# Loading the memory and the first weight unit in alternating column halves, with products of zeros on TensorE until the memory is there

## What is computed

```python
kv_m = rms_norm(mem, mem_norm_g[l]) @ w_mem_kv[l]
k_m, v_m = jnp.split(kv_m, 2, axis=-1)
...
h = rms_norm(x, norm_g[l])
proj = h @ w_in[l]
```

## Time and profile before

| | |
|---|---|
| median of 3 executions | 1388.79 us (1387.9 to 1390.12) |
| the profiled execution's own time | 1389.63 us |
| its span, first to last instruction | 1387.8 us |
| PE, DVE, ACT, POOL busy | 1349.3, 971.3, 742.3, 57.0 us |
| mean granted TensorE clock | 0.997 |
| HBM read | 224.05 MB |

### The profile page before, as it was taken

The page is one execution under the profiler, slowest core; times in us unless marked ns, Lnnn a source line. Parts: engine busy times, 40 slices in busy tenths (PEclk is TensorE's granted clock), DMA queues, the critical chain, the costliest instruction groups (busy, mean ns, idle before and its releaser), DMA issues.

```text
span 1387.8 us, 17865 instructions
## 1 busy us (share of the span) xinstructions
PE 1349.3 (97%) x7119; PEld 1146.4 (83%) x7119; DVE 971.3 (70%) x1230; ACT 742.3 (53%) x1045; POOL 57.0 (4%) x46
## 2 busy tenths in 40 slices
PE   7999999989999999999999999999999999999998
PEld 6978888978887898887877888879888887788886
DVE  6689776699776498747876555457796678565644
ACT  6864766764684565544454444346744444454432
POOL 1002000001100001000000000000100000000000
PEclk9999999999999999999999999999999999999999
DMA  8554335544343655434445554455643344476553
GB/s 294 186 169 155 100 122 182 183 129 155 113 144 131 224 176 174 147 126 144 152 152 182 182 182 168 166 180 185 200 157 123 120 143 146 145 221 186 189 180 110
DMA packets 139697, 226.25 MB, mean 163 GB/s; under 512 B 8096, under 2 KB 54880, under 8 KB 139488
## 3 DMA queue, kind: packets, MB, share of 16 engines
q1 hardware_dynamic: 137952, 222.49, 48.8%
q10 hardware_dynamic: 1664, 2.63, 0.5%
HBM read 224.05 MB, written 1.05 MB: 162 GB/s over the span
## 4 chain that ended last, share of the span: by engine, by line
PE 80%; DVE 12%; ACT 4%; issue 2%; POOL 1%; DMA 0%; SPq 0%; ACTq 0%; DVEq 0%
PE gp L613 61%; PE gp L602 7%; PE mp L585 4%; DVE arena L1466 4%; DVE wt_rest L1472 3%; PE mp L896 2%; PE mp L715 1%; DVE arena L1472 1%; PE mp L782 1%; DVE arena L1956 1%; POOL rs_out L2222 1%; DVE arena L1469 1%; PE mp L757 1%; ACT arena L1048 1%; PE mp L743 0%
## 5 line engine op out<-in xcount | busy, mean ns | idle before, releaser
L1472 DVE TENSOR_TENSOR wt_rest<-wt,wt_hi 128x1024 fp32r<-128x1024 f32 x156 | 184.1, 1221 | 77.6 <-ACT wt_hi L1080 76.9
L1080 ACT ACTIVATE wt_hi<-wt 128x1024 fp32r<-128x1024 f32 x156 | 156.8, 1054 | 101.9 <-DMA wt<-in_ffn_up 51.0
L1080 ACT ACTIVATE mix_hi<-wt 128x1024 fp32r<-128x1024 f32 x136 | 139.7, 1062 | 103.3 <-PE gp L613 58.4
L1472 DVE TENSOR_TENSOR wt_rest<-wt,mix_hi 128x1024 fp32r<-128x1024 f32 x136 | 160.5, 1220 | 34.2 <-ACT mix_hi L1080 33.3
L613 PE MATMUL gp<-wt_rest,mix_hT_hi 128*128 128x512 f32 x384 | 149.8, 390 | 0.0
L613 PE MATMUL gp<-mix_hi,mix_hT_hi 128*128 128x512 f32 x352 | 140.7, 400 | 4.6 <-DVE wt_rest L1472 3.7
L613 PE MATMUL gp<-wt_hi,hT_hi 128*128 128x512 f32 x352 | 140.2, 398 | 4.8 <-DVE wt_rest L1472 4.0
L613 PE MATMUL gp<-wt_hi,hT_rest 128*128 128x512 f32 x352 | 137.5, 391 | 0.0
L613 PE MATMUL gp<-mix_hi,mix_hT_rest 128*128 128x512 f32 x352 | 137.3, 390 | 0.0
L613 PE MATMUL gp<-wt_rest,hT_hi 128*128 128x512 f32 x352 | 137.2, 390 | 0.0
L1080 ACT ACTIVATE first_hi<-wt 128x1024 fp32r<-128x1024 f32 x104 | 106.4, 1061 | 49.1 <-PE gp L613 36.7
(11 more groups left out here) (331 smaller groups left out, 2913.7 us busy)
## 6 DMA issues: line engine op xcount, KB each, us to landing
wt<-in_w_in SPq DMA_DIRECT2D x100, 1024.0 KB, 5.0
wt<-in_ffn_gate SPq DMA_DIRECT2D x44, 512.0 KB, 4.0
wt<-in_ffn_up SPq DMA_DIRECT2D x44, 512.0 KB, 5.0
wt<-in_w_out SPq DMA_DIRECT2D x20, 1024.0 KB, 5.0
wt<-in_ffn_down SPq DMA_DIRECT2D x20, 1024.0 KB, 5.1
wt<-in_w_mem_kv SPq DMA_DIRECT2D x8, 1024.0 KB, 6.2
wt<-in_w_branch_pool SPq DMA_DIRECT2D x4, 1024.0 KB, 5.1
wt<-in_w_branch_ret SPq DMA_DIRECT2D x4, 1024.0 KB, 5.0
```

What stands on the lines that cost most here:

```text
L1080: nc.scalar.activation(rounded_part(u)[:, k:k + nk, :], wt[:, u % SLOTS, k:k + nk, :], ACT.Copy)\
L1472: return nc.vector.tensor_tensor(o, i0, i1, ALU.subtract)
```

## The change

SP loads the memory as two column halves of both tiles and unit 0 as two half units, in the order memory half 0, weight half 0, memory half 1, weight half 1. A new semaphore first_part stands for weight half 0. The steps memT0 to memT3 are renumbered (q, t) = divmod(i, 2) on all engines. DVE handles column half 0 fully (two multiplications, then remainder of memory, weight half 0, remainder of memory, weight half 1) ahead of column half 1. ACT rounds weight half 0 ahead of the second memory tile and weight half 1 ahead of column half 1. In layer 0 PE waits for the remainders of column half 0 alone ahead of unit 0, and of half 1 ahead of unit 1. DVE clears a 128x128 tile first, and PE multiplies it with itself four times ahead of the gain columns and four times behind them, into a PSUM bank that nothing else uses yet.

```diff
--- before.py
+++ after.py
@@ -285,6 +285,7 @@
         first_lower, flip = flips[:, 0:P], flips[:, P:2 * P]
         hst, hst_off = region(a_st, TT, NH, P), region(a_sto, NH, P)
         restart = region(a_rm, 1024)
+        idle_tile = region(a_o, P)
         QT, KT = region(a_QT, NH_A, S), region(a_KT, 4, S)
         sco, prT = region(a_S, NH_A, 384), region(a_PT, NH_A, 384)
         msc, mprT = region(a_S, NH, TT, MEM), region(a_PT, NH, 4, P)
@@ -373,6 +374,7 @@
 
         loaded = {n: sem("loaded_" + n) for n in ("ident", "const", "const2", "gain0", "rows", "rows_b", "x", "mem0", "mem1", "gain1", "early", "late", "ba", "flips", "lower", "masks")}
         w_loaded = [sem(f"w_loaded{i}") for i in range(SLOTS)]
+        first_part = sem("first_part")
         w_used = sem("w_used")
         group_read = [sem(f"group_read{i}") for i in range(2)]
         step_done = sem("step_done")
@@ -517,9 +519,13 @@
         @block.sync
         def _(sp):
             sp.dma_start(const[:, 0:P], w["shape_constants"][:, 0:P]).then_inc(loaded["ident"], 16)
-            for t in range(TT):
-                sp.dma_start(region(a_S, TT, D)[:, t], w["mem"][0, t * P:(t + 1) * P, :]).then_inc(loaded[f"mem{t}"], 16)
-            for u in range(len(UNITS)):
+            for q in range(2):
+                sp.dma_start(region(a_S, TT, D)[:, :, G * q:G * q + G], w["mem"][0][:, G * q:G * q + G].rearrange("(t p) d -> p t d", p=P))\
+                    .then_inc(loaded[f"mem{q}"], 16)
+                (dst, src), = unit_loads(0)
+                sp.dma_start(dst[:, PART_K * q:PART_K * q + PART_K], src[:, PART_K * q:PART_K * q + PART_K])\
+                    .then_inc(first_part if q == 0 else w_loaded[0], 16)
+            for u in range(1, len(UNITS)):
                 if u == 2:
                     sp.dma_start(x[:, :, :], w["x"][0].rearrange("(t p) d -> p t d", p=P)).then_inc(loaded["x"], 16)
                     for name, src in (("norm_g", "norm_g"), ("mix_pre", "mix_pre_norm_2"), ("ffn_pre", "ffn_pre_norm_2"),
@@ -679,13 +685,19 @@
                     transposes(names(i), [src[:, t, (4 * q + j) * P:(4 * q + j + 1) * P] for j in range(4)],
                                (sig("x_normed"), 2 * n + t + 1))
 
+            def keep_clock(count):
+                for _ in range(count):
+                    nc.tensor.matmul(gp[:, 3, 0:P], idle_tile, idle_tile, start=True, stop=True)
+            pe.wait_ge(sig("idle_tile"), 1)
+            keep_clock(4)
             pe.wait_ge(loaded["ident"], 16)
             begin("colM", (loaded["gain0"], 16))
             end(nc.tensor.transpose(bank("colM")[:, 0:16], small[0:16, 0:P], ident[0:16, 0:16]))
+            keep_clock(4)
             for i in range(4):
-                t, q = divmod(i, 2)
+                q, t = divmod(i, 2)
                 transposes(f"memT{i}", [region(a_S, TT, D)[:, t, (4 * q + j) * P:(4 * q + j + 1) * P] for j in range(4)],
-                           (loaded[f"mem{t}"], 16))
+                           (loaded[f"mem{q}"], 16))
 
             def columns():
                 begin("colA", (loaded["rows"], 16 * 5))
@@ -696,11 +708,11 @@
 
             for l in range(DEPTH):
                 s = lambda n: f"A{l}.{n}"
-                split_units(s("KM"), 1, tile_ready=lambda t: (sig("mem_scaled"), 4 * l + TT * (t + 1)))
+                split_units(s("KM"), 1, tile_ready=lambda t: (sig("mem_scaled"), t + 1 if l == 0 else 4 * l + TT * (t + 1)))
                 if l == 0:
                     columns()
                     pe.wait_ge(sig("cleared"), 1)
-                split_units(s("KM"), 1)
+                split_units(s("KM"), 1, tile_ready=lambda t: (sig("mem_scaled"), 4 * l + TT + t + 1 if l == 0 else 4 * l + 4))
                 x_transposes(lambda i: s(f"xT{i}"), xs, l)
                 split_units(s("VM"), 2)
                 pe.wait_ge(sig("first_split"), TT * (l + 1))
@@ -1059,7 +1071,7 @@
             def round_weights(count):
                 while rounded[0] < count:
                     u, k, nk = PARTS[rounded[0]]
-                    act.wait_ge(w_loaded[u % SLOTS], unit_value[u])
+                    act.wait_ge(*((first_part, 16) if u == 0 and k == 0 else (w_loaded[u % SLOTS], unit_value[u])))
                     i = mixer_index(u)
                     if u == last_unit(f"A{DEPTH - 1}.O1"):
                         act.wait_ge(*summed(f"A{DEPTH - 1}.Z0"))
@@ -1089,9 +1101,11 @@
 
             act.dma_start(small[0:16, 0:P], w["mem_norm_g"].rearrange("l (k p) -> (l k) p", p=P)).then_inc(loaded["gain0"], 16)
             for i in range(4):
-                t, q = divmod(i, 2)
+                q, t = divmod(i, 2)
+                if i == 2:
+                    round_weights(2)
                 act.wait_ge(sig("mem_gained"), i + 1)
-                if i == 3:
+                if i == 1:
                     round_weights(1)
                 nc.scalar.activation(mem_hi[:, t, 4 * q:4 * q + 4, :], mem_s[:, t, 4 * q:4 * q + 4, :], ACT.Copy).then_inc(sig("mem_rounded"), 1)
             round_weights(parts_until(1))
@@ -1513,22 +1527,22 @@
                 return nc.vector.tensor_copy(o, i)
 
 
+            nc.vector.memset(idle_tile, 0.0).then_inc(sig("idle_tile"), 1)
             v(nc.vector.memset(minus_half[:, :], -0.5))
 
             dve.wait_ge(*computed("colM"))
             evac(copy(cols[:, 0:16], bank("colM", 16)), "colM")
-            for i in range(4):
-                t, q = divmod(i, 2)
-                dve.wait_ge(*computed(f"memT{i}"))
-                mul(mem_s[:, t, 4 * q:4 * q + 4, :], bank(f"memT{i}", 4, P),
-                    col("mem_norm_g", 0)[:, 4 * q:4 * q + 4][:, :, None].to_broadcast([P, 4, P])).then_inc(sig("mem_gained"), 1)
-            for i in range(4):
-                t, q = divmod(i, 2)
-                if i == 2:
-                    weight_rests(1)
-                dve.wait_ge(sig("mem_rounded"), i + 1)
-                sub(mem_rest[:, t, 4 * q:4 * q + 4, :], mem_s[:, t, 4 * q:4 * q + 4, :], mem_hi[:, t, 4 * q:4 * q + 4, :].bitcast(F))\
-                    .then_inc(sig("mem_scaled"), 1)
+            for q in range(2):
+                for t in range(TT):
+                    dve.wait_ge(*computed(f"memT{TT * q + t}"))
+                    mul(mem_s[:, t, 4 * q:4 * q + 4, :], bank(f"memT{TT * q + t}", 4, P),
+                        col("mem_norm_g", 0)[:, 4 * q:4 * q + 4][:, :, None].to_broadcast([P, 4, P])).then_inc(sig("mem_gained"), 1)
+                for t in range(TT):
+                    dve.wait_ge(sig("mem_rounded"), TT * q + t + 1)
+                    sub(mem_rest[:, t, 4 * q:4 * q + 4, :], mem_s[:, t, 4 * q:4 * q + 4, :], mem_hi[:, t, 4 * q:4 * q + 4, :].bitcast(F))\
+                        .then_inc(sig("mem_scaled"), 1)
+                    if q == 0:
+                        weight_rests(t + 1)
             weight_rests(parts_until(1))
             dve.wait_ge(sig("mem_squared"), 1)
             r = rstd(small[:, 364:366], 2, 1.0 / D, 1e-6)
```

## The result

The changed kernel takes 1392.53 us (median of 9, 1391.37 to 1392.81) against 1389.34 (9 runs, 1386.09 to 1390.14) for the kernel before: ratio 1.0027, 95% interval 1.0019 to 1.0036. It is 3.2 us slower, where 0.9 us faster was forecast. The profiled execution has a span of 1390.7 us against 1387.8, so the profiles show 2.9 us of it.

A forecast was written before the change was run, and what follows sets the result against it. The prediction took PE's row of products, fed by ACT's and DVE's lists, as the bound; PE's earlier start and clock gain ended in a wait at unit 3, leaving -0.9 us from 1388.79: 1387.9 us, range 1385.9 to 1390.2.

The forecast's parts named there:

- the first view: Whole span: PE busy 97%; time is saved only where PE starts its products earlier and stays ahead of DVE and ACT.
- (a): SP's first loads: halves land at 5.4, 6.6, 8.0 and 9.3; three extra issues cost zero, bounds 0 and 1.3 us.
- (b): Eight zero products on PE before memory lands: four take 1.8 us; cost zero, up to 0.3 us if memory landed earlier.
- (c): ACT and DVE order: PE starts unit 0 1.7 us earlier, ACT is 1.7 us later, unit 3 ready at 31.85.
- (d): PE's row: unit 1 at 16.4 at full clock; a new wait for unit 3, 29.9 to 31.9, absorbs earlier start and clock.
- the 0.9 us of the sum: PE's start of unit 3: 31.9 in place of 32.8, a gain of 0.9 us kept until the end.
- Rival D: The clock falls in the new wait at unit 3: slow products cost 2.4 us, net +1.5, 1390.3 us; chance 0.08.
- the 3.54 of the earlier trace: Kernel before, wait before 287.96: 3.54 us, followed by 6.8 us at the low clock and 5.3 us of slow products.
- Rival E: First loads: every half costs a whole MB's 2.7 us, unit 3 is 3.9 later, net +3.0, 1391.8 us; chance 0.04.
- Rival B: PE decides: its whole gain of start and clock arrives, -3.4 us, 1385.4 us; chance 0.08.
- the limit of 1.35 us: Unit 4: load lands at 34.60, DVE's remainder ends at 36.9, so no gain above 1.35 us passes.
- What the prediction took from that page on transposes: PE's clock before unit 0: transposes do not count as busy; 3.7 us of them left products slow at 12.25.

The follow-up runs named there:

- e2_rows_late: The changed kernel with PE's two transposes of gain rows moved from between units 0 and 1 to behind unit 1; 1389.19 us against 1388.88, ratio 1.0002.
- e3_fill_wait: The changed kernel with 14 further products of zeros on PE between unit 0 and the first transpose of gain rows; 1390.15 us against 1388.88, ratio 1.0011.
- e6_order_only: The changed kernel with the old whole loads put back, new order of work and zeros kept; 1392.28 us against 1389.04, ratio 1.0022.
- e11_unit2_first: The kernel before with zeros throughout, gain rows behind unit 1, and DVE's unit 2 remainders ahead of its gain-row copies; 1387.25 us against 1389.33, ratio 0.9985.
- e4_zeros_only: The kernel before with the eight products of zeros and nothing else; 1388.68 us against 1388.88, ratio 0.9996.
- e9_old_order_zeros: The kernel before with gain rows behind unit 1, the eight zeros and 14 more behind the memory's transposes; 1388.75 us against 1389.04, ratio 0.9998.
- e7_gains_early: The changed kernel with gain rows behind unit 1 and DVE's multiplications of memory half 1 moved earlier; 1389.98 us against 1389.04, ratio 1.0004.
- e13_change_mended: The changed kernel with gain rows behind unit 1 and DVE's unit 2 remainders ahead of its gain-row copies; 1389.82 us against 1389.33, ratio 1.0011.
- e1_no_zeros: The changed kernel without its eight products of zeros; 1391.6 us against 1388.88, ratio 1.0025.

## Why the prediction was wrong, point by point

**What bounds the kernel, and the first view.** Right as far as it went: the loss is in PE's row of products, and the 4.1 us at unit 4 are carried to the end but for the 0.95 us that come back at layer 1 and 0.3 elsewhere.

**(a) The landings** were mis-sized. The first half of the memory came up to 0.8 late, the second half of unit 0 at 10.1 (e2_rows_late) to 10.6 where 9.3 was summed. That was within the bound of 1.3 that I gave for SP's three extra issues of 0.42 to 0.61 each, and I had taken zero. Not all of it is the halves' doing: unit 0 loaded whole landed anywhere between 9.1 and 10.0 in the profiles of the other kernels.

**(b) Zeros**: right to cost them nothing on the path. Four took 2.07 us and not 1.8.

**(c) ACT's list** was the sound part: "ACT is 1.7 us later" came out as 2.4, of which 0.7 came with the landing. Unit 0 started 1.0 and not 1.7 earlier for the same reason.

**(c) again, the step that failed: a wait put at nothing.** I went from ACT's squares through its copies of the memory straight to the rounding of unit 2 and asked only who waits for that. The copies themselves have a waiter: PE's transposes of the gain rows, which stand between units 0 and 1 and reuse the memory's PSUM banks. The text on PE, "unit 1 at 16.4, bound by the remainder at 16.33", passes over them. By the numbers of (c) and (d) PE ends unit 0 between 16.0 and 18.9, and ACT's first copy ends at 18.9+1.7=20.6: a wait of 1.7 to 4.6 us, which could have been summed from what was in the text. It measured 3.66 us and set unit 1 back by 2.05 us against the kernel before; the slow products behind it cost 2.05 more. e2_rows_late shows that this alone is the loss.

**(d) Both the start and the clock end in the wait at unit 3.** Right in place and kind, though shown only once the rows were moved: the wait ends at 32.46 where 31.9 was summed and is 1.71 us long for 2.0. About 0.4 us of it is my repair's, so the agreement of the two lengths is in part luck. Nor does the 0.9 us of the sum come even so: unit 3 starts 0.4 earlier than in the kernel before (32.46 for 32.83) and unit 4 0.2. In the changed kernel itself this wait does not come up, as unit 2 is far later.

**The clock.** Rival D had the mechanism (a new wait, then slow products, 2.4 us) at the wrong wait, and so with too small a chance. It measured 2.05 us, and e3_fill_wait showed the cause. Its place was unit 1 and its wait 3.66 us, longer than the 3.54 of the earlier trace rows, so by those rows it was likely there. The two parts, 2.05 of wait and 2.05 of clock, are the 4.1. Rival E, the halves dear, has the nearest total (1391.8) for a wrong reason: e6_order_only is as slow with whole loads. Rival B, that PE's whole gain arrives, does not hold for the change even without the new wait: in e2_rows_late unit 1 starts 2.75 us earlier than in the kernel before (17.30 for 20.05) and unit 4 only 0.2. In the old order of ACT and DVE most of it does arrive: in e11_unit2_first unit 1 starts 2.0 us earlier (18.02) and unit 4 1.5. That unit 4 lands at 34.60 was loose as well: where ACT waited for that load, it took it between 32.5 and 35.3, and the limit of 1.35 us that I drew from it did not hold, as e11_unit2_first gains 1.5.

**The page's rule.** The Trainium skill (TensorE: Matmul & The Clock Gate, Why this matters for your kernels) says that idle gaps between bursts bring the low clock back. The trace agrees behind 3.66 us, but at layer 1 a wait of 3.52 us in e2_rows_late did not bring it back. That the zeros would start the products at the full level, as the prediction worked out by that page, did not come either: in the change the first three are slow. What the prediction took from that page on transposes stands in its Part 4: PE-mode transpose, and no run tests it by itself. An earlier start on PE only lengthens the gap if the next thing that PE needs has not moved.

## What to carry to other kernels

When a list on one engine moves, every instruction in it has a waiter of its own. Go through the moved list one entry at a time, name who waits for each and its slack, and count both movements, the producer's later and the waiter's earlier. Waits for a reused bank do not look like data flow and are easily passed over. The waits of 2.4 to 4.0 us in TensorE's row were mostly paid twice here, once as idle time and once as products at half rate behind them, so start work earlier on one engine only if what it needs next is ready earlier too.

## What the runs showed of the hardware that was not expected

The same eight zeros raised the clock at about 5 to 7 us in eight profiles (e3_fill_wait, e4_zeros_only and e9_old_order_zeros among them) and not before the first real products in three (the change, e2_rows_late, e7_gains_early, where transposes still took 1.97 us for eight). The clock's answer to one and the same stretch is not fixed from profile to profile. The wait of about 3.5 us at 284 to 288 shows the same: 6.8 us at the low level in the kernel before, 3.4 in the changed one, and none in e2_rows_late:

```profile
280.00:292.00 12.00, 8.48 (x38) 6.76 (x37) 11.76 (x14) 7.98 (x10) 0.00 (x0) 1.00 0.51 174
```

That is worth 0 to 2.6 us per execution, and it is of the size of the spread of the kernel before, 1386.1 to 1390.1; that it makes this spread is not shown. Waits of 1.70 to 1.73 us were followed by products at full spacing in five kernels; slow instructions followed the one of 2.43 us, and those of 2.04 (e13_change_mended) and 2.12 us (e3_fill_wait) ahead of the memory's last transposes. The fall can come late: behind 3.92 us (e1_no_zeros) and 4.02 us (e4_zeros_only) two or three products still ran at full spacing first. And a first load of 0.5 MB landed anywhere between 3.8 and 5.0 us after its issue.
